# Delta rule: gates of both kinds in one tile, turned and worked out on 128 partitions, and half-array products for 64 moving columns only

## The reference, cut to what matters

```python
beta = jax.nn.sigmoid(b)
g = -jnp.exp(a_log) * jax.nn.softplus(a + dt_bias)
gc = jnp.cumsum(g, axis=-1)                      # inside a chunk
a_mat = jnp.where(strict, (k * beta) @ k.T * decay(gc), 0.0)
t_mat = lax.linalg.triangular_solve(a_mat, eye, ...)
u, w = t_mat @ (v * beta), t_mat @ (k * beta * exp(gc))
# step over the chunks:
v_new = u - w @ state
o = (q * exp(gc)) @ state + qk @ v_new
state = state * exp(g_last) + (k * exp(g_last - gc)).T @ v_new
```

## Time and profile before

| | us |
|---|---|
| median of 3 runs | 2956.2 (2953.94 to 2957.23) |
| profiled execution, its own time | 2954.82 |
| its span | 2952.7 |
| TensorE busy in the span | 2815.0 (95%) |
| VectorE, ScalarE, GpSimd busy | 1013.2, 1099.1, 1371.9 |
| mean granted clock of TensorE | 0.982 |

### The profile page before, as it was taken

The page is one execution under the profiler, slowest core; times in us unless marked ns, Lnnn a source line. Parts: engine busy times, 40 slices in busy tenths (PEclk is TensorE's granted clock), DMA queues, the critical chain, the costliest instruction groups (busy, mean ns, idle before and its releaser), DMA issues.

```text
span 2952.7 us, 39046 instructions
## 1 busy us (share of the span) xinstructions
PE 2815.0 (95%) x15534; PEld 2193.7 (74%) x15534; DVE 1013.2 (34%) x1906; ACT 1099.1 (37%) x1644; POOL 1371.9 (46%) x1073
## 2 busy tenths in 40 slices
PE   7899899999989999998899999999999899899999
PEld 5776678888756788887566676788887866678887
DVE  3024441113485512125465564311222034432112
ACT  4245442223345423233333433422334245443221
POOL 3366634444454344444243242444455367544443
PEclk9999999999999999999899999999999999999999
DMA  4222122333431133224111110233323232023322
GB/s 119 86 72 65 44 72 90 96 99 100 100 72 44 58 100 100 89 96 108 30 44 44 30 44 30 72 100 100 99 86 92 86 72 65 29 87 99 100 92 78
DMA packets 271762, 227.92 MB, mean 77 GB/s; under 512 B 30100, under 2 KB 259220, under 8 KB 271620
## 3 DMA queue, kind: packets, MB, share of 16 engines
q1 hardware_dynamic: 260880, 216.29, 24.3%
q10 hardware_dynamic: 10740, 9.65, 1.4%
HBM read 223.61 MB, written 2.30 MB: 77 GB/s over the span
## 4 chain that ended last, share of the span: by engine, by line
PE 84%; DVE 6%; POOL 4%; ACT 4%; issue 1%; DMA 0%; ACTq 0%; DVEq 0%; POOLq 0%
PE bank L1756 47%; PE bank L1667 17%; PE bank L2041 6%; PE bank L1815 5%; POOL w_lo L555 3%; PE bank L1710 1%; PE bank L1792 1%; ACT w_hi L688 1%; POOL arena L577 1%; PE bank L1866 1%; PE bank L1970 1%; PE bank L1998 1%; PE bank L1882 1%; PE bank L1983 1%; PE bank L1845 0%
## 5 line engine op out<-in xcount | busy, mean ns | idle before, releaser
L555 POOL TENSOR_TENSOR w_lo<-raw,w_hi 128x512 fp32r<-128x512 f32 x808 | 1067.8, 1354 | 1264.2 <-ACT w_hi L688 1264.2
L688 ACT ACTIVATE w_hi<-raw 128x2048 fp32r<-128x2048 f32 x202 | 385.5, 1908 | 478.8 <-PE bank L1756 423.3
L1756 PE MATMUL bank<-h_hi,w_hi 128*128 128x512 f32 x1024 | 400.8, 391 | 0.0
L1756 PE MATMUL bank<-h_hi,w_lo 128*128 128x512 f32 x1024 | 398.4, 389 | 0.0
L1756 PE MATMUL bank<-h_lo,w_hi 128*128 128x512 f32 x1024 | 398.4, 389 | 0.0
L1756 PE MATMUL bank<-g_hi,w_hi 128*128 128x512 f32 x1024 | 398.3, 389 | 0.0
L1756 PE MATMUL bank<-g_lo,w_hi 128*128 128x512 f32 x1024 | 398.3, 389 | 0.0
L1756 PE MATMUL bank<-g_hi,w_lo 128*128 128x512 f32 x1024 | 398.3, 389 | 0.0
L1667 PE MATMUL bank<-h_hi,w_hi 128*128 128x512 f32 x784 | 332.4, 424 | 6.9 <-POOL w_lo L555 4.6
L1667 PE MATMUL bank<-h_lo,w_hi 128*128 128x512 f32 x784 | 323.0, 412 | 0.0
L1667 PE MATMUL bank<-h_hi,w_lo 128*128 128x512 f32 x784 | 319.6, 408 | 0.0
(11 more groups left out here) (233 smaller groups left out, 3773.0 us busy)
## 6 DMA issues: line engine op xcount, KB each, us to landing
raw<-in_mlp_w SPq DMA_DIRECT2D x128, 1024.0 KB, 5.3
raw<-in_a_w_in SPq DMA_DIRECT2D x48, 512.0 KB, 5.2
raw<-in_c_w_in SPq DMA_DIRECT2D x32, 512.0 KB, 5.4
raw<-in_a_w_in SPq DMA_DIRECT2D x12, 1024.0 KB, 5.1
raw<-in_b_w_in SPq DMA_DIRECT2D x18, 256.0 KB, 4.1
raw<-in_a_w_out SPq DMA_DIRECT2D x4, 1024.0 KB, 4.8
raw<-in_b_w_in SPq DMA_DIRECT2D x4, 1024.0 KB, 5.4
arena<-bias_scratch ACTq DMA_DIRECT2D x16, 256.0 KB, 3.5
```

The lines of the kernel that those rows point to most:

```text
L555: ins = nc.gpsimd.tensor_tensor(w_lo[s][:, k, :], raw[s][:, k, :], w_hi[s][:, k, :].bitcast(F32), ALU.subtract)
L688: nc.scalar.activation(w_hi[s][:], raw[s][:], ACT.Copy).then_inc(w_hi_done, 1)
L1756: mm = nc.tensor.matmul(lin_bank[j][:], w[s][:, c, P * j:P * j + P], a[:, c, :], start=c + z == 0, stop=c == CT - 1 and z == 2)
```

## The change

- The chunk `cab` now has the columns b on partitions 0 to 7 and the columns a on 32 to 39 of one tile; the second tile's product is gone.
- VectorE scales these 40 rows once. TensorE turns them, after 12 fillers, into four blocks of 128 tokens x 40 in bank 2, and the gates are worked out on 128 x 32 (tokens x chunks and heads). The 8 dt_bias and 8 a_log values are spread over 128 partitions by their DMA. The running sums become a product with a triangle of ones (`m_past`), the last value of each chunk one with `ones`, both at filler 34.
- ScalarE's tanh for beta stands behind the exponentials; the convolutions of head 0 are reordered, and the loads and order of its tanh with them.
- The rows of a head are spread by 8 products whose weights are one column repeated 128 times, with the identity as moving operand, in the place of two products of 8 rows with 512 moving columns; `head_sel` is gone.
- All products of 128 or more moving columns that went through `in_halves` are plain full-array products (`norm_sums`, `key_products`, W, wt, vn, state, o, state increment, output sum). Those of TW keep the halves.

```diff
-                    for s in range(2):
-                        load(n, r[:, :, P * s:P * s + 8], rows(w, 4096 + 8 * s, 8))
-                        load(n, r[:, :, P * s + 8:P * s + P], rows(w, 0, P - 8))
+                    load(n, r[:, :, 0:8], rows(w, 4096, 8))
+                    load(n, r[:, :, 8:GATE_A], rows(w, 0, GATE_A - 8))
+                    load(n, r[:, :, GATE_A:GATE_A + 8], rows(w, 4104, 8))
+                    load(n, r[:, :, GATE_A + 8:CW], rows(w, 0, CW - GATE_A - 8))
...
-                act.dma_start(gate_in[C8, :], c_gates).then_inc(cmask_loaded, 16)
+                act.dma_start(gate_in, c_gates[0:1, :].to_broadcast([P, 2 * C_HEADS])).then_inc(cmask_loaded, 16)
                 round_ahead(n0)
-                act.wait_ge(copied, copy_first[i] + 1)
...
+                nc.scalar.activation(neg_a, gate_in[:, 0:C_HEADS], ACT.Exp).then_inc(gate_exp, 1)
...
+                act.wait_ge(gates_summed, 1)
+                nc.scalar.activation(flat(gc_col), bank[3][:, 0:32], ACT.Copy).then_inc(cols_copied, 1)
+                nc.scalar.activation(flat(beta_g), bank[3][:, 0:32], ACT.Exp).then_inc(col_exp, 1)
+                nc.scalar.activation(flat(e_last), bank[4][:, 0:32], ACT.Exp).then_inc(col_exp, 1)
+                act.wait_ge(col_exp, 3)
+                nc.scalar.activation(flat(k_decay), flat(k_decay), ACT.Exp).then_inc(col_exp, 1)
+                nc.scalar.activation(beta_col, gate_cols[:, :, 0:C_HEADS], ACT.Tanh, scale=0.5).then_inc(gate_exp, 1)
+                c_tanh(i, [(0, 0)])
...
-                c_tanh(i, [(0, 0), (0, 1), (0, 2)])
-                act.wait_ge(col_exp, 3)
-                nc.scalar.activation(k_decay, k_decay, ACT.Exp).then_inc(col_exp, 1)
+                c_tanh(i, [(0, 1), (0, 2)])
...
+                dve.wait_ge(lin_done, t0 + 1)
+                nc.vector.tensor_tensor(gate_rows, lin_bank[t0 % 2][0:GATE_A + C_HEADS, :], rs[0:GATE_A + C_HEADS, :],
+                                        ALU.mult).then_inc(copied, 2)
...
+                dve.wait_ge(cols_turned, 1)
+                nc.vector.tensor_tensor(gz, gate_cols[:, :, GATE_A:GATE_A + C_HEADS],
+                                        gate_in[:, C_HEADS:].unsqueeze(1).to_broadcast([P, *by_head]),
+                                        ALU.add).then_inc(gate_z, 1)
+                dve.wait_ge(gate_exp, 3)
+                nc.vector.tensor_scalar(flat(gu), flat(ge), 1.0, None, ALU.add).then_inc(gate_ln, 1)
...
-                for c in range(NB):
-                    ins = nc.vector.tensor_tensor_scan(gc_row[C8, P * c:P * c + P], ones[C8, :], gr[:, P * c:P * c + P],
-                                                       0.0, ALU.mult, ALU.add)
-                ins.then_inc(gates_ready, 1)
...
+                nc.vector.scalar_tensor_tensor(gr, gr, -1.0, neg_a.unsqueeze(1).to_broadcast([P, *by_head]), ALU.mult,
+                                               ALU.mult).then_inc(gates_ready, 1)
...
+                dve.wait_ge(cols_copied, 1)
+                dve.wait_ge(col_exp, 2)
+                nc.vector.tensor_tensor(flat(k_decay), bank[4][:, 0:32], flat(gc_col), ALU.subtract).then_inc(col_exp, 1)
+                c_copy(i, 0, 0)
+                conv_steps(i, 0, 0, range(4))
+                dve.wait_ge(gate_exp, 5)
+                nc.vector.tensor_scalar(flat(beta_col), flat(beta_col), 1.0, 0.5, ALU.add, ALU.mult).then_inc(gates_ready, 1)
+                dve.wait_ge(gates_ready, 2)
+                nc.vector.tensor_tensor(flat(beta_g), flat(beta_g), flat(beta_col), ALU.mult)
+                silu(0, 0)
                 c_copy(i, 0, 1)
-                for k in (0, 1):
-                    conv_steps(i, 0, k, range(4))
-                silu(0, 0)
+                conv_steps(i, 0, 1, range(4))
+                silu(0, 1)
                 c_copy(i, 0, 2)
                 conv_steps(i, 0, 2, range(4))
-                silu(0, 1)
                 c_copy(i, 0, 3)
                 silu(0, 2)
...
+                    mm.then_inc(lin_done, 2 if CHUNKS[n][0] == "cab" else 1)
...
-                product(n0, tile0[n0] + 1, H, CT, 0, 24, None, 0, None)
...
-                fill(0, 0, 60)
+                fill(0, 0, 12)
+                pe.wait_ge(copied, copy_first[i] + 2)
+                for c in range(NB):
+                    mm = nc.tensor.transpose(gate_cols[:, c, :], gate_rows[:, P * c:P * c + P],
+                                             ident[0:GATE_A + C_HEADS, 0:GATE_A + C_HEADS])
+                mm.then_inc(cols_turned, 1)
+                fill(0, 12, 34)
                 pe.wait_ge(gates_ready, 1)
-                for k, rows in enumerate((gc_row, beta_row)):
-                    for c in range(NB):
-                        mm = nc.tensor.transpose(bank[2 + k][:, C_HEADS * c:C_HEADS * c + C_HEADS],
-                                                 rows[C8, P * c:P * c + P], ident[C8, C8])
-                mm.then_inc(cols_turned, 1)
-                fill(0, 60, 84)
-                pe.wait_ge(cols_copied, 2)
-                pe.wait_ge(cmask_loaded, 32)
-                in_halves(bank[4][:, 0:32], m_last, gc_col.rearrange("p c h -> p (c h)"), start=True,
-                                 stop=True).then_inc(last_spread, 1)
-                fill(0, 84, 96)
+                nc.tensor.matmul(bank[3][:, 0:32], m_past, flat(gr), start=True, stop=True)
+                nc.tensor.matmul(bank[4][:, 0:32], ones, flat(gr), start=True, stop=True).then_inc(gates_summed, 1)
+                fill(0, 34, 96)
...
-                    in_halves(bank[2][:], head_sel[C8, h, :], gc_row[C8, :], start=True, stop=True)
-                    in_halves(bank[3][:], head_sel[C8, h, :], beta_row[C8, :], start=True,
-                                     stop=True).then_inc(rows_spread, 1)
+                    else:
+                        pe.wait_ge(cols_copied, 1)
+                        pe.wait_ge(gates_ready, 2)
+                    for k, col in ((2, gc_col), (3, beta_col)):
+                        for c in range(NB):
+                            mm = nc.tensor.matmul(bk4(k)[:, c, :], col[:, c, h:h + 1].to_broadcast([P, P]), ident, start=True,
+                                                  stop=True)
+                    mm.then_inc(rows_spread, 1)
...
-                            mm = in_halves(bk4(3)[:, c, :], atl[k % 3][:, c, :], Tm[:, c, :], start=True, stop=True)
+                            mm = nc.tensor.matmul(bk4(3)[:, c, :], atl[k % 3][:, c, :], Tm[:, c, :], start=True, stop=True)
...
-    masks[M_LAST] = (r == P - 1) * np.ones((1, P))
+    masks[M_PAST] = r <= c
```

More of the change, by code:

```diff
@@ L50 @@
 CLAMP = 44.0
+GATE_A = 32
 B_PAIRS = B_HEADS // 2
@@ L66 @@
 M_ID, M_ONES, M_HALVES = 0, 1, 2
-M_CAUSAL, M_DECAY, M_LAST, M_LEVEL = 3, 4, 5, 6
+M_CAUSAL, M_DECAY, M_PAST, M_LEVEL = 3, 4, 5, 6
 LEVELS = 7
@@ L291, in trunk @@
         fresh()
-        gc_row, beta_row = part(TOK), part(TOK)
-        head_sel = part(C_HEADS * P).rearrange("p (h n) -> p h n", h=C_HEADS)
         cmask = part((NMASK - M_DECAY) * P).rearrange("p (k n) -> p k n", n=P)
-        gate_in = part(2)
-        neg_a = part(1)
+        gate_in = part(2 * C_HEADS)
+        neg_a = part(C_HEADS)
         def cols():
             return part(NB * C_HEADS).rearrange("p (c h) -> p c h", c=NB)
-        gc_col, beta_col, g_last, e_last, k_decay, beta_g = (cols() for _ in range(6))
+        gc_col, beta_col, e_last, k_decay, beta_g = (cols() for _ in range(5))
+        gz, ge, gu, gl_, gd, gr = (cols() for _ in range(6))
         cx = [part(TOK) for _ in range(2)]
@@ L1473, in c_gates_steps @@
-                nc.vector.tensor_scalar(gz, gz, gate_in[C8, 1:2], None, ALU.add).then_inc(gate_z, 1)
-                dve.wait_ge(gate_exp, 1)
-                link(nc.vector.tensor_scalar(beta_row[C8, :], beta_row[C8, :], 1.0, 0.5, ALU.add, ALU.mult))
-                nc.vector.tensor_copy(head_sel[C8], ident[C8, 0:C_HEADS].unsqueeze(2).to_broadcast([C_HEADS, C_HEADS, P]))
-                dve.wait_ge(gate_exp, 4)
-                nc.vector.tensor_scalar(gu, ge, 1.0, None, ALU.add).then_inc(gate_ln, 1)
@@ new lines, in c_gates_steps @@
+                dve.wait_ge(gate_exp, 3)
+                nc.vector.tensor_scalar(flat(gu), flat(ge), 1.0, None, ALU.add).then_inc(gate_ln, 1)
+                dve.wait_ge(gate_ln, 1)
+                link(nc.vector.tensor_scalar(flat(gd), flat(gu), 1.0, None, ALU.subtract))
+                link(nc.vector.tensor_scalar(flat(gr), flat(gd), 1e-30, None, ALU.max))
+                link(nc.vector.reciprocal(flat(gr), flat(gr)))
+                link(nc.vector.tensor_tensor(flat(gr), flat(gr), flat(ge), ALU.mult))
@@ L2149, in mixer_c @@
                     for c in range(NB):
-                        mm = in_halves(bk4(4)[:, c, :], k_beta[:, c, :], Um[:, c, :], start=True, stop=True)
+                        mm = nc.tensor.matmul(bk4(4)[:, c, :], k_beta[:, c, :], Um[:, c, :], start=True, stop=True)
                     mm.then_inc(wt_done, 1)
```

(10 more changed lines are left out.)

65 lines of the change are left out of this document (18 added, 47 removed).

## The result

The kernel after takes 2917.87 us (median of 4 runs, 2914.73 to 2921.46), beside 2956.72 us before: ratio **0.9877**, 95% interval 0.9864 to 0.9889. Run again beside its own variants it took 2920.89 (ratio 0.9879, 0.9863 to 0.9896) and 2919.38 us (0.9884, 0.9868 to 0.9901). Forecast was 2914.0, range 2902 to 2934. Its profiled execution took 2918.57 us with a span of 2916.7; before it was 2954.82 and 2952.7, so the traces have 36.0 us to explain.

What follows compares the result with a forecast made beforehand. TensorE, busy 95% of the span, was taken as the bound, so only its queue or its idle stretches count. From 2954.8 us, steady state takes 23.8 and setup 17.0, giving 2914.0 us, range 2902 to 2934.

Steps and rivals of the forecast that it cites:

- Full step 0.112: Full fp32 records with 128 moving columns step at 0.112 us, as pairs of halves do now, at no cost.
- Rival 1: Weight loads surface: full records step at up to 0.218 us instead of 0.112, giving 2999 us; chance 0.07.
- Switches and levels: Six levels per head lose W's half-array switching: 0.25 us per level, about 0.3 in the first, 1.57 per head.
- 0.24, not 0.34: Sign behind W: a filler starts 0.24 us after the first filler there, not 0.34.
- Tail: From wt to the next head's turns: 1.5 us gained to osum, 0.25 from key products and fillers, 1.75 per head.
- Rows at nothing: Row spread: TensorE's savings count for nothing, since VectorE works without a gap up to the turn of Um.
- Head 7: The last head waits for ScalarE and VectorE in every level already, so gains only about 0.6 us in its tail.
- Setup: Stretch before the first head's turn: smaller gate operations and less switching gain 17 us, between 11 and 21.
- 1401: Time in us of the first norm sums in setup, taken from 1399.5 to 1402.5, against 1417.4 before.
- rival 2: Chains take over: TensorE waits for ScalarE and VectorE, a head gives 1.5 us, setup 13, total 2931; chance 0.2.

Runs made afterwards that it cites:

- e4: Kernel after with TW and its partner product (64 moving columns) on the full array too: 2955.54 us, ratio 1.0001.
- e1: Kernel before with mixer C's products of 128 or 512 moving columns as plain full-array products, gates as before: 2936.55 us, ratio 0.9935.
- e2: Kernel after with every product made full-array turned back into two half-array products, gates as after: 2942.78 us, ratio 0.9961.
- e10: Kernel after with GpSimd's first masked product of each head held back until VectorE has written Um: 2914.68 us, ratio 0.9867.
- e3: Kernel before with W alone (4 products of 128 columns in each of 6 levels) as full-array products: 2944.79 us, ratio 0.9970.

## Why the prediction was right, step by step

**Full step 0.112: right** (0.111). Rival 1, up to 0.218, is dead. With it falls, for this kernel, the rule that a load overlaps only into other row groups (Trainium skill, TensorE: Matmul & The Clock Gate, "What overlaps and what doesn't"). The load time of the Trainium skill (the same page, "LDWEIGHTS (loading the stationary operand)"), 107 ns for 128 columns by an estimate from columns / 1.2, agrees in size with e4, where 64 and 128 moving columns both step at 0.112.

**Switches and levels: right in kind, too low.** Behind W the first filler starts 0.03 us after W's last record, where it was 0.20, and the second 0.31 after the first, where it was 0.34. So the sign "0.24, not 0.34" did not come, but from W's last record to the second filler it is 0.34 instead of 0.54, the 0.2 that the prediction had summed for exit and slow fillers. TW waits for ScalarE, as said, 0.96 behind W's last record (0.97 forecast). A level gives 0.27 to 0.30, the second 0.46, where 0.25 was taken, and 0.11 comes ahead of the first W. From the turn to wt a head gives 26.08 - 24.11 = 1.97 us, not 1.57: a step mis-sized by a quarter.

**Tail: too high.** From wt to osum 12.33 us became 11.20, a gain of 1.14 where 1.5 stood; key products and their fillers gave 0.13, not 0.25. A full record that waited for its operand is followed after 0.21 us, not 0.11:

```profile
1506.72 0.39 PE L2156 MATMUL bank<-arena 128*128 128x128 f32 x2
1506.86 0.48 PE L1660 MATMUL bank<-h_lo,w_hi 128*128 128x512 f32 x1
1507.25 0.49 PE L2161 MATMUL bank<-arena 128*128 128x128 f32 x2
...
1508.77 1.12 PE L2169 MATMUL bank<-sq,com 128*128 128x512 f32 x2 [0.57 <-ACT sq L1091]
```

L2156 is 0.39 with both records, L2161 0.49 behind its wait. Seven such products per head lose 0.07 to 0.10 each, 0.68 together; the 0.05 of a slow first pair of halves would have made 0.35. The difference, 0.33, is near the missing 0.36, but that it is the cause is not shown: osum itself stands behind ScalarE. From the start of ScalarE's last copy of vn to osum it is 1.85 us in both traces (1528.90 to 1530.75, 1506.92 to 1508.77), and behind wt that copy comes only 1.13 us earlier.

**Rows at nothing: the step that failed.** VectorE does set the turn of Um, as said, but its length did change: from the turned keys to the turn 9.81 us became 10.20. Two of its steps beside GpSimd are longer, L1549, which writes Um (above, 1.67), than L1556 (1.47), and L1591 (after) than L1598 (before):

```profile
1515.55 1.63 DVE L1591 TENSOR_TENSOR g_lo<-ss,g_hi 128x512 fp32r<-128x512 f32 x1
```

```profile
1537.67 1.45 DVE L1598 TENSOR_TENSOR g_lo<-ss,g_hi 128x512 fp32r<-128x512 f32 x1
```

That is 0.38 us per head lost. e1 and e2 take the two apart ("stretch" is VectorE's from its first step on the turned keys to the end of the one that writes Um, all in us; GpSimd's is the median of its 48 masked products):

| kernel | GpSimd's masked product | step that writes Um | step of g_lo | stretch |
|---|---|---|---|---|
| before | 1.10 | 1.47 | 1.45 | 9.76 |
| e1 products only | 1.10 | 1.47 | 1.62 | 9.92 |
| e2 gates only | 1.29 | 1.67 | 1.47 | 9.98 |
| after | 1.30 | 1.67 | 1.63 | 10.14 |
| e10 masks held back | 1.29 | 0.69 | 1.63 | 9.16 |

The step of g_lo is a matter of phase, and comes with the products: it starts 0.38 us behind the start of GpSimd's split before and 0.21 after, and ends 1.83 and 1.84 behind it. The step of Um is not. It starts 0.68 us behind GpSimd's first masked product in both, but that product itself takes longer:

```profile
1543.47 1.60 POOL L649 TENSOR_TENSOR arena<-arena 128x512 f32<-128x512 f32 x1 [0.25 <-DVE arena L1551]
```

```profile
1521.55 1.80 POOL L650 TENSOR_TENSOR arena<-arena 128x512 f32<-128x512 f32 x1 [0.25 <-DVE arena L1544]
```

All four steps end 0.55 us behind the end of the GpSimd operation that they run beside. The masked product is the same line with the same shapes in all kernels, and slower in all that have the new gates. The change moves the tiles in `arena`; whether this is why was not tested. e10 shows the cause of the longer Um step in place: with GpSimd out of the way L1550 takes 0.69.

Sum per head: 1.97 + 1.14 + 0.13 - 0.38 = 2.86, against 3.3; seven heads 19.9, against 23.2. Head 7 gave nothing, against 0.6: from its turn to osum it takes 33.29 us before and 33.23 after.

**Setup: mechanism right, 17 was high.** Measured 12.1, 14.1 and 15.7 in three executions. TensorE stood 2.6 us for the split (2.8 said), and at the two sums of the gates the 34 fillers were the later ones (in the first execution gates ready 1379.0, TensorE there at 1380.9; in the other two by 1.5 and 0.1). The norm's sums come 34.8, 33.6 and 32.1 us after the norm's record; forecast 1401 - 1370.4 = 30.6. That the first execution has them at 1401.3, almost the 1401 of the forecast, is luck: its norm lay 3.9 us earlier. What I priced too low are two things I had named. The clock's fall, which I had put only behind the norm's sums, came in two of three executions at the first fillers (0 to 2.7 us). And GpSimd's split lay beside the whole second convolution: 2.9 us in L1445 and 0.3 in the silu behind it, where my value 1401 of a span 1399.5 to 1402.5 had taken half of that. From the norm's sums to the turn of Um it took 21.7, 20.9 and 20.9, against 21.7 before; 0.6 less was said.

The two sums were too high by 3.9 us (heads) and 1.3 to 4.9 (setup), 8.8 in the profiled pair, of which the 3.9 that lie ahead of the change gave back nearly half. The time came out 4 to 7 above the forecast, between it and rival 2 (2931): the chains that this rival names took part of the gain, at the places above.

## What to carry to other kernels

A half-array product among full-array ones pays some 0.3 us at its edges and buys nothing once 128 columns move; at 64 it is twice as fast and worth them, above all where it waits for its operand anyway. When a chain is called unchanged, look which of its steps run beside GpSimd, for moving everything by a few us changes what meets what, and GpSimd's own operation can have changed its length with no edit to its line (1.10 to 1.29 us here); holding one GpSimd operation back until the critical step was done gave 0.85 us per head. Two edits that live on the same idle stretch don't add up.

## What the runs showed of the hardware

- VectorE's operation with all its operands in SBUF waits beside GpSimd's (with two, 0.69 becomes 1.4 to 1.7 us and a fused step 0.75 becomes 1.66 to 1.84; with one, 128x32, 0.18 becomes 1.21), while one with an operand in a bank, L1432 or L1542, keeps its 0.68 in the same stretch. The Trainium skill (SBUF — State Buffer, "SBUF: two separate sides") has it as an exclusive lock on a shared port pair, held for a whole instruction, the later one blocked; the lengths agree, and GpSimd's own 1.26 growing to 1.75 agrees with either engine being the later one.
- GpSimd's masked product, one line with one shape, takes 1.10 us in before, e1 and e3, and 1.29 in the kernels with the new gates; the cause is open.
- A full fp32 record costs 0.112 us whether 64 or 128 columns move; 512 cost 0.429.
- A record behind a wait delays its successor by 0.07 to 0.10 us.
- The same idle stretch of 2.6 us was followed by 6.8, 3.4 and 0 us at 1.2 GHz in three executions of one kernel.
